# A two-layer hybrid decoder step: first halves of block weights loaded from DRAM into the sums, the last of GpSimd's sums made by VectorE

## The reference

```
for i in range(2):
    x = x + 0.5 * swiglu(rmsnorm(x, norm_ffn1[i]), w_ffn1_gate[i], w_ffn1_up[i], w_ffn1_down[i])
    h = rmsnorm(x, norm_mix[i])
    x = x + (latent attention(h, paged cache) if i == 0 else short gated convolution(h))
    x = x + 0.5 * swiglu(rmsnorm(x, norm_ffn2[i]), w_ffn2_gate[i], w_ffn2_up[i], w_ffn2_down[i])

def swiglu(h, wg, wu, wd):
    return (jax.nn.silu(h @ wg) * (h @ wu)) @ wd
```

## Time and profile before

| | us |
|---|---|
| median of 3 runs | 2507.07 (2506.56 to 2524.66) |
| the profiled execution, its own time | 2519.46 |
| its span in the profile | 2517.6 |
| TensorE matmul busy in the span | 2346.6 (93%) |
| VectorE busy | 1657.7 (66%) |
| ScalarE busy | 1165.5 (46%) |
| GpSimd busy | 487.6 (19%) |
| mean granted TensorE clock | 0.98 |

### The profile page before, as it was taken

How to read it: one execution, slowest core, us unless ns; L and a number is a source line. 1 busy time by engine, 2 the same in 40 slices (tenths; PEclk the granted TensorE clock), 3 DMA queues, 4 the chain that set the end, 5 groups by cost and what they waited for, 6 DMA issues and landing times.

```text
span 2517.6 us, 47212 instructions
## 1 busy us (share of the span) xinstructions
PE 2346.6 (93%) x17889; PEld 2254.5 (90%) x17889; DVE 1657.7 (66%) x2599; ACT 1165.5 (46%) x2162; POOL 487.6 (19%) x342
## 2 busy tenths in 40 slices
PE   7798999999999999999898999899999999899998
PEld 7798899976899999999898999898999999789898
DVE  7776765556455555547876667867766656877764
ACT  4445444364455555534445444445544223444542
POOL 0333330000000000000333330343430000334340
PEclk9999999989999999999999999899999999999999
DMA  4677764311111111203676664577773333577772
GB/s 136 157 179 185 182 173 125 87 47 30 45 44 47 49 45 42 60 26 93 168 191 175 179 167 119 134 184 193 185 181 101 90 93 93 134 184 185 190 195 85
DMA packets 417696, 313.29 MB, mean 124 GB/s; under 512 B 34624, under 2 KB 372630, under 8 KB 417480
## 3 DMA queue, kind: packets, MB, share of 16 engines
q1 hardware_dynamic: 401748, 253.66, 34.0%
q0 software_dynamic: 15552, 56.63, 12.9%
q10 hardware_dynamic: 180, 0.11, 0.0%
HBM read 194.27 MB, written 2.87 MB: 78 GB/s over the span
## 4 chain that ended last, share of the span: by engine, by line
PE 19%; DMA 15%; DVE 7%; issue 4%; POOL 4%; ACT 2%; DVEq 0%; ACTq 0%; SPq 0%; POOLq 0%
DMA wsum75b<-raw 7%; PE ps L552 4%; PE ps L556 4%; PE ps L554 4%; DMA raw<-in_w_ffn_up 3%; PE ps L946 2%; DMA wsum<-raw 2%; PE ps L948 2%; PE ps L947 2%; POOL wsum L734 2%; DMA raw<-in_w_ffn_down 2%; POOL wsum L732 2%; DVE w_lo L683 1%; ACT w_hi L669 1%; DVE hs L778 1%
## 5 line engine op out<-in xcount | busy, mean ns | idle before, releaser
L946 PE MATMUL ps<-hs,w_hi 128*128 128x260 f32 x1440 | 417.0, 290 | 65.1 <-ACT gate_t L1013 25.5
L947 PE MATMUL ps<-hs,w_hi 128*128 128x260 f32 x1440 | 411.4, 286 | 0.0
L948 PE MATMUL ps<-hs,w_lo 128*128 128x260 f32 x1440 | 411.1, 285 | 0.0
L946 PEld LDWEIGHTS ps<-hs,w_hi 128*128 128x128 f32 x1440 | 275.6, 191 | 77.6 <-DVE w_lo L673 38.8
L947 PEld LDWEIGHTS ps<-hs,w_hi 128*128 128x128 f32 x1440 | 276.4, 192 | 0.0
L948 PEld LDWEIGHTS ps<-hs,w_lo 128*128 128x128 f32 x1440 | 275.8, 192 | 0.0
L2071 ACT ACTIVATE ksq<-ps 128x384 f32<-128x384 f32 (+1 forms) x384 | 146.8, 455 | 196.6 <-PE ps L2024 196.6
L946 PE MATMUL ps<-hs,x_hi 128*128 128x260 f32 x688 | 202.2, 294 | 34.8 <-DVE x_lo L653 13.9
L734 POOL TENSOR_TENSOR wsum<-wsum,raw 128x512 f32<-128x512 f32 x108 | 206.3, 1911 | 8.5
L947 PE MATMUL ps<-hs,x_hi 128*128 128x260 f32 x688 | 198.3, 288 | 0.0
L948 PE MATMUL ps<-hs,x_lo 128*128 128x260 f32 x688 | 198.2, 288 | 0.0
(11 more groups left out here) (409 smaller groups left out, 6410.3 us busy)
## 6 DMA issues: line engine op xcount, KB each, us to landing
raw<-in_w_ffn_gate SPq DMA_DIRECT2D x88, 512.0 KB, 4.1
raw<-in_w_ffn_up SPq DMA_DIRECT2D x88, 512.0 KB, 3.9
raw<-in_w_ffn_down SPq DMA_DIRECT2D x64, 512.0 KB, 4.5
wsum<-raw SPq DMA_DIRECT2D x56, 512.0 KB, 3.5
wsum<-raw POOLq DMA_DIRECT2D x56, 512.0 KB, 4.8
wsum75b<-raw SPq DMA_DIRECT2D x52, 512.0 KB, 3.4
wsum75b<-raw POOLq DMA_DIRECT2D x52, 512.0 KB, 5.0
cache<-in_cache_latent SPq DMA_DIRECT2D x128, 128.0 KB, 2.0
```

The lines of the kernel that those rows point to most:

```text
L946: nc.tensor.matmul(o, hi[:, kc], mh[:, xc], start=start and k == 0, stop=False, skip_group_check=goes_on)
L947: nc.tensor.matmul(o, hi[:, kc], ml[:, xc], start=False, stop=False, skip_group_check=goes_on)
L948: mm = nc.tensor.matmul(o, lo[:, kc], mh[:, xc], start=False, stop=k == KH - 1, skip_group_check=goes_on)
```

## The change

Three things are changed, all in the FFN blocks of kinds S and D.

First, the copy within SBUF is replaced by two loads from DRAM, of the first halves of both weights (256 KB each), straight into the sums tile. They stand on SP between the load of the first weight and the load of the second. They wait for the same release of the sums tile as the copy did, and, new, for the accumulation of the block before (`sums_added`). GpSimd now waits itself for both weights before it issues the accumulation.

Second, s3 is made by VectorE (`last_sum`), between its work on the next block's first weight and `first_made`; GpSimd keeps s6.

Third, two orders are changed. On ScalarE `keep_second` stands ahead of the rounding of a finished pair. On VectorE, in blocks after the first, `pair_mix` stands behind `m75_lo` and `second_made` and not ahead of them, and `first_begun` ahead of the rest of a pair and not behind it.

```diff
@@ -706,32 +706,38 @@
             nc.vector.tensor_tensor(ring(LO, bk, 0, 2)[:, 0:w], raw[:, bk.raw_slot(0), 0:w], ring(HI, bk, 0, 2)[:, 0:w],
                                     ALU.subtract).then_inc(part_lo_made, bk.size)
 
-        def sums_begin(sp, bk):
-
-            for j in range(2):
-                bk.loaded(sp, j)
+        def sums_begin(sp, bk, first, second):
+
             if bk.b == 4:
                 sp.wait_ge(set_made, own_sets(bk.at, KH))
                 sp.wait_ge(part_used, blocks[bk.at][2].done)
             elif bk.b > 4:
                 sp.wait_ge(part_lo_made, blocks[bk.at][bk.b - 2].end(M75, 2))
-            r = bk.raw_slot(0)
-            sp.dma_start(bk.sums()[:].rearrange("p (h c) -> p h c", h=2), raw[:, r:r + 2, 0:bk.width]).then_inc(sums_in, 16)
+            if bk.s:
+                sp.wait_ge(sums_added, 16 * bk.s)
+            dst = bk.sums()[:].rearrange("p (h k c) -> p h k c", h=2, c=P)
+            sp.dma_start(dst[:, 0], first[:, 0:KH, :]).then_inc(sums_in, 16)
+            sp.dma_start(dst[:, 1], second[:, 0:KH, :]).then_inc(sums_in, 16)
 
         def weight_sums(pool, bk):
 
-            g1, g2 = bk.raw_half(0, 0), bk.raw_half(0, 1)
             w = bk.width
-            s6, s3, s5 = wsum63[:, 0:w], wsum63[:, w:2 * w], bk.sums()[:, w:2 * w]
+            s6, s5, g1 = wsum63[:, 0:w], bk.sums()[:, w:2 * w], bk.raw_half(0, 0)
             ahead = blocks[bk.at][bk.b - 1] if bk.b > 3 else blocks[bk.at - 1][PLAIN0 - 1] if bk.at else None
-            pool.wait_ge(sums_in, 16 * (bk.s + 1))
+            for j in range(2):
+                bk.loaded(pool, j)
+            pool.wait_ge(sums_in, 32 * (bk.s + 1))
             pool.dma_start(bk.sums()[:], bk.raw_row(1), accum_op=ALU.add).then_inc(sums_added, 16)
             if ahead:
                 pool.wait_ge(part_lo_made, ahead.end(M63, 2))
             pool.wait_ge(sums_added, 16 * (bk.s + 1))
             nc.gpsimd.tensor_tensor(s6, s5, g1, ALU.add).then_inc(sums_made, 1)
-            pool.wait_ge(sums_made, 2 * bk.s + 1)
-            nc.gpsimd.tensor_tensor(s3, s6, g2, ALU.add).then_inc(sums_made, 1)
+
+        def last_sum(dve, bk):
+
+            s6, s3 = wsum63[:, 0:bk.width], wsum63[:, bk.width:2 * bk.width]
+            dve.wait_ge(sums_made, 2 * bk.s + 1)
+            nc.vector.tensor_tensor(s3, s6, bk.raw_half(0, 1), ALU.add).then_inc(sums_made, 1)
 
 
         def part_of(f, x, n=1):
@@ -843,8 +849,16 @@
             for j in range(2):
                 if u0 + j:
                     load_unit(sp, Unit(u0 + j), (gw, uw)[j][:, :, 0:P], UC, KD)
+
+            def weights(bk, j):
+                if bk.out:
+                    return dw[:, BASES[bk.c]:BASES[bk.c] + KD, (2 * bk.d + j) * P:(2 * bk.d + j + 1) * P]
+                return (gw, uw)[j][:, :, bk.f * P:(bk.f + 1) * P]
+
             for bk in blocks[at][1:]:
                 for j in range(bk.loads):
+                    if j and bk.kind in "SD":
+                        sums_begin(sp, bk, src, weights(bk, 1))
                     if bk.raw + j >= RAW:
                         raw_free(sp, bk.raw + j)
                     if bk.plain:
@@ -852,14 +866,8 @@
                         dst = raw[:, bk.raw_slot(0), 0:LAST * P].rearrange("p (k c) -> p k c", c=P)
                         sp.dma_start(dst, src).then_inc(weights_in[bk.raw_slot(0)], 16)
                         continue
-                    if bk.out:
-                        k0, d0 = BASES[bk.c], (2 * bk.d + j) * P
-                        src = dw[:, k0:k0 + KD, d0:d0 + P]
-                    else:
-                        src = (gw, uw)[j][:, :, bk.f * P:(bk.f + 1) * P]
+                    src = weights(bk, j)
                     sp.dma_start(bk.raw_row(j).rearrange("p (k c) -> p k c", c=P), src).then_inc(weights_in[bk.raw_slot(j)], 16)
-                if bk.kind in "SD":
-                    sums_begin(sp, bk)
 
         def ffn_pool(pool, i):
             for bk in blocks[FFN_AT[i]][3:PLAIN0]:
@@ -1025,9 +1033,9 @@
                 m75_hi(act, bk)
                 keep_first(bk)
                 m4_hi(act, bk)
+                keep_second(bk)
                 if done:
                     last_hi(act, done) if done.last else pair_hi(act, done)
-                keep_second(bk)
                 plain_hi(act, nxt) if nxt.plain else first_hi(act, nxt)
                 keep_third(bk)
                 if not nxt.plain:
@@ -1160,22 +1168,25 @@
                 early = bk.b > 3
                 if early:
                     after(old)
-                    if done and not done.last:
-                        pair_mix(dve, done)
                 m75_lo(dve, bk)
                 second_made(bk)
-                m4_lo(dve, bk)
                 if not early:
+                    m4_lo(dve, bk)
                     pair_mix(dve, done)
                     first_begun(bk)
                     pair_lo(dve, done)
                     first_lo(dve, nxt)
                     plain_hid(old)
                 else:
+                    if done and not done.last:
+                        pair_mix(dve, done)
+                    m4_lo(dve, bk)
+                    first_begun(bk)
                     if done:
                         last_lo(dve, done) if done.last else pair_lo(dve, done)
-                    first_begun(bk)
                     plain_lo(dve, nxt) if nxt.plain else first_lo(dve, nxt)
+                if not nxt.plain:
+                    last_sum(dve, nxt)
                 first_made(bk)
                 up_made(bk)
                 if bk.out:
@@ -1210,6 +1221,7 @@
             scaled_dve(dve, at, 3)
             set_mix(dve, at, 3)
             first_lo(dve, own[3])
+            last_sum(dve, own[3])
             set_lo(dve, at, 2)
             set_lo(dve, at, 3)
             m63_lo(dve, own[3])
```

## The result

The changed kernel takes 2566.70 us (median of 4 runs, 2559.83 to 2574.19), against 2513.84 us for the kernel before (4 runs, 2506.56 to 2524.66). The ratio is 1.0207, with a 95% interval of 1.0153 to 1.0262: about 2% slower. The profiled execution took 2559.83 us, span 2558.0, 40.4 us over the span before. The forecast was 2434, range 2390 to 2500.

The account below looks back on a forecast made before the run. A two-block loop of loads and sums was taken to bound the kernel, at 11.33 us a block, with TensorE waiting. A new 10.6 us turn over 100 blocks saves 73 us: 2507 - 73 = 2434 us, range 2390 to 2500.

Parts of the forecast that it names:

- A new turn, over one block: FFN blocks: accumulation, half loads, second weight's load and next accumulation form a one-block loop of 10.6 us (10.1 to 12.0).
- queueing term: In the one-block loop, delay of the second weight's data behind 512 KB of half loads: taken as 0.5 us, 0 to 1.9 possible.
- GpSimd's issue: In the one-block loop, time from the second weight's landing to the issue of GpSimd's accumulation: 0.29 us.
- The old loop: Two-block loop of load, copy, accumulation, sums and slot release: 22.35 us, falling to 17.6 and no longer binding.
- The copy goes: Copy into the sums tile leaves the two-block loop: 3.20 us and 0.05 before its issue saved; two 256 KB loads added per block.
- s3 moves: s3 goes from GpSimd (2.16 us) to VectorE (0.69 us): 1.5 us less in the two-block loop.
- The changed orders: Pair blocks, ScalarE and VectorE: waits before M75 shrink, but nothing is counted while the DMA turn sets the pace.
- VectorE's load: Pair blocks rise from 10.5 to 11.2 us of VectorE work, some 0.6 late; taken as hidden, at most 17 us in all.
- Beginnings and ends: FFN starts and ends: extra s3 costs 2.8 us, other gains and losses in block 3; set at 0, give or take 6.
- reading of the clock: Granted clock in the FFN windows is 0.99 or 1.00, the full 2.4 GHz but for a few stretches.
- The fourth: Rival: next block's first weight load falls on the accumulation, making it 6.2 us and the turn 11.9; 57 us slower, 2564; chance 0.10.
- the third rival: Half loads not hidden: their queueing costs 1.2 us, the turn is 11.3, one loop replaces another; no change, 2507; chance 0.10.

## Why the prediction was wrong

**The step that failed is "A new turn, over one block"**: its terms are right in kind and order, and too small in sum. The loop exists, it took the place of the old one, and it sets the pace. I gave it 10.6 us; it takes 11.7. By the prediction's own rule it decides at 11.33, so an error of 1.1 us in a sum of 10.6 turned a gain of 3% into a loss of 2%. Term by term, from the chain shown above and as means of the 100 turns:

| term | predicted | chain | mean |
|---|---|---|---|
| landing to SP's first issue | 0.05 | 0.06 | 0.06 |
| two issues | 0.94 | 1.02 | 1.07 |
| second weight | 3.9 + 0.5 | 5.31 | 5.26 |
| landing to the accumulation's issue | 0.29 | 0.52 | 0.53 |
| accumulation | 4.9 | 4.5 to 4.9 | 4.83 |
| sum | 10.6 | 11.4 to 11.8 | 11.75 |

*The second weight* is most of the error: 5.26 us, where the sum had 4.4. The queueing term in it was 1.1 to 1.2, not 0.5: with the quarter-size half loads the second weight lands after 4.21 in the mean of the same turns (median 4.07) in place of 5.26 (median 5.25). The first weight behind it adds only 0.2, by the run that held it back (mean 5.10, median 5.06). The other 0.3 is in the load itself. My 3.9 was the median of all 88 loads of `in_w_ffn_up`, 20 of which stand outside the windows; in the windows of the kernel before the second weight took 4.4 in the median and 4.6 in the mean.

My 0.5 had no working: I knew that 0 to 1.9 was possible and scaled. Rows that I had gave better. In a block without pauses the DMA engines moved 209 GB/s; 524,288 bytes of half loads take 2.5 us at that rate, and SP's two issues give them about 1.0 us of start, which leaves 1.5, near the 1.1 to 1.2. Likewise the quarter-size ones need 0.6 us, less than their start, and add next to nothing. With 1.5 the sum was 11.6, which meant no gain or a loss. This working is an estimate made after the result.

*GpSimd's issue* takes 0.53 in place of 0.29. The instruction now stands behind waits on three semaphores and not one. That they are the cause was not tried, and one thing speaks against their number alone: with the second weight first, only the last of the three is still waited for, and it takes 0.57.

**The old loop.** "The copy goes" was right in direction: with the half loads behind the second weight and nothing else changed the kernel gains 42 us (2469.7 against 2511.7). "s3 moves" was right in its duration (0.69) and wrong in its credit: I took 1.5 us out of the loop, and on the kernel before slower transfers and a later start of s3 gave nearly all of it back. With the second weight first the same move is worth 34 us with the old orders and 39 with the new. Argued from this, and not shown: the old loop did not alone set the pace there, and a faster s3 let its transfers fall on others. In the change's place s3 on VectorE may even cost: 2575.8 against 2555.8 with the old orders, though the two ratios, from two chips, touch at 1.0227. Why it would is open.

**The changed orders** were counted at nothing "when the DMA turn sets the pace". In the turn that was nearly right (9 us less, within the intervals); the prediction's remark that "were the turn gone, both would matter" had the wrong sign. They cost 27 us on the kernel before. With the second weight first they cost 12 (s3 on VectorE) and 17 (on GpSimd), each within overlapping intervals but with the same sign. Two consequences were seen as predicted: the wait on `keep_second` went to nothing, and the M75 waits from 34 to 1. What I did not follow was the pair behind them, and this is argued from the waits: mixing, rounding, rest and the next M12 form one queue, and starting it later by the 1.2 us of `m75_lo` delays the next block.

**VectorE's load** was no limit. Its busy time in the windows rose by 32 us and not by the 69 of the 100 sums, since its other work got shorter: the rests of line 653 on `w_hi` from 1696 to 1437 ns, while GpSimd's busy time halved. That the second is the cause of the first was not tried. Beginnings and ends: 3 us outside the windows, within the 6 allowed. The prediction's reading of the clock was off in one window, which had 0.98 and not 0.99 or 1.00; no term hangs on it.

**The rivals.** The fourth gave 2564 and the time is 2566.7, but that is luck: its mechanism is another. It asked for accumulations of 6.2 us; they take 4.6 in the median and 4.8 in the mean, since the first weight has only 1.1 us left (median) when they begin. That mechanism appears in full only when the first weight is held back (6.0, and 2676.9). The rule of the Trainium skill cited beside it (DMA: Bandwidth & Descriptors, "Issuing engines are not separate DMA queues") is borne out by that run, and by the changed kernel in the other sense: with the loads nearly through, the accumulation is faster than before (4.6 against 4.9). What happened is the third rival, taken further. It set the queueing term at 1.2, about what it is, and stopped at 11.3 and "no change"; the 0.3 of the load itself, the 0.24 of GpSimd's issue and the 0.13 of SP's issues carry on past 11.33. The sum's upper end of 12.0 held the measured 11.75. The range did not, since it was cut short of the third rival. An honest range from the bounds stated would have reached 2574.

## What to carry to other kernels

When a transfer is moved ahead of a load that somebody waits for, its bytes divided by the measured rate, less the time it has before that load is issued, are a first estimate of what is added to the load's landing (here 1.5 us against 1.1 to 1.2 measured). Where the moved transfer also waits for the consumer of that load, a loop is closed: sum it in full, and if the sum comes near the present pace the sign is open and the range must reach over it. Here the sum was 6% under the pace, and 10% too small. The cheap guard is to put what waits for the last step behind what the next step needs: here two lines on SP, 2448 in place of 2567.

A part that saves time in a chain's row need not save any (s3: 0 or 39 us, by what else binds). Take the parts one at a time before keeping a bundle: the best versions here have the second weight first and the old orders, with one semaphore or two, 3% faster than before.

## What the runs showed of the hardware

- A load of 512 KB (`in_w_ffn_up`) lands after 3.9 us in the median in the kernel before and 4.0 with the second weight first. With 512 KB issued 1 us earlier on the same queue it lands after 5.0 to 5.3, with 128 KB after 4.0.
- An accumulation of 512 KB within SBUF takes at least 4.5 us. With a load of 512 KB issued just before it (the run that holds the first weight back) it takes 6.0 in the median and up to 7.5.
- From the landing of what was waited for to the issue of GpSimd's accumulation 0.29 us passed in the chain before, with one semaphore to wait for, and 0.52 with three.
- SP takes 0.37 to 0.50 us for most issues of such a load, in the rows shown, and 0.05 between two. Single ones took longer, one 1.74 us (1743.51 in the changed kernel).
